# Staging the attention queries on GpSimd in a two-layer hybrid decoder step

## The chip, the cores and the metric

The kernel runs on one core of one Trainium2 chip. A core has five engines that each work through their own list of instructions in order and meet only at semaphores: TensorE (PE in the profile, with its weight loads shown apart as PEld), VectorE (DVE), ScalarE (ACT), GpSimd (POOL) and SyncE (SP), which here issues every DMA. The metric is the device time of one execution in microseconds (us). Lower is better.

## The reference, cut to what matters

One step of a small decoder with two layers: 1024 prompt tokens and 8 sequences of 8 new tokens, model width 1024. The part that matters is the attention of the prompt.

- The first layer has three groups of windowed attention, with 8 heads of 64 features each and dilations 1, 4 and 16. Each group works on blocks of 128 queries against at most 256 keys.
- The second layer has one group with 16 query heads and 4 key heads, the same window of 128, and a sink value per head.

```python
def banded_attn(q, k, v, n_steps):              # blocks of 128 queries
    kb, vb = key_blocks(k), key_blocks(v)       # own block and the one before
    s = einsum('nbqgrd,nbkgd->nbgrqk', qb, kb) * (hd ** -0.5)
    pexp, m, l = _masked_softmax_parts(s, valid)   # exp(s - max), max, sum
    o = einsum('nbgrqk,nbkgd->nbqgrd', pexp, vb)
    return o, m, l
```

Everything else (projections, a state-space layer, the feed-forward parts, the sample attentions) is not touched by the change.

## The kernel before, in words

**Slots.** All weights come as 111 slots of 1.1 MB. For each slot SP loads the raw weights (`feed`, L353), GpSimd splits them into a high and a low part (`split_slot`: a cast on L645, a subtraction on L647), and TensorE multiplies with them. There are two split buffers, so GpSimd's split of slot n waits until TensorE has finished slot n-2. GpSimd does nothing but these splits. SP's load of slot n+1 waits for the end of the split of slot n, since there is one raw buffer.

**The attentions.** The first layer runs, for each of its three groups (g = 0, 1, 2), two value slots, four query and key slots, and then `attend(g, 8 heads)`. The second layer runs `attend(0, 16 heads)` once, after its slot W_VC. An attention goes over 8 tiles of 128 queries. A tile has one step for each pair of heads: 4 steps in the first layer, 8 in the second. In g = 0, in the odd tiles of g = 1 and in the second layer a step sees 256 keys (128 in the first tile); the even tiles of g = 1 and all of g = 2 see 128.

**One step k of a tile, engine by engine.** A query has to be scaled and laid out so that each head's 64 features stand alone among zeros in a 128-row operand. That is the staging: ACT copies 64 x 128 pieces from XA into QST (first layer) or QCST (second), two per step, on L1285, and raises `q_ready`. Then

- PE makes the scores of both heads (L845), raising `s_mm`;
- DVE adds the mask (L1785), takes the negated maximum (L1790) and, in the second layer, takes the minimum with the sink (L1793);
- ACT makes the two exponentials with their sums (L1300);
- PE transposes them (L856), ACT copies the result to SBUF (L1308), and PE multiplies with the values (L870);
- DVE scales the tile's outputs (L1756 to L1758, L1770) and, in the first layer, SP stores them to `og` (L459 to L467).

**The order on each engine is written out by hand.** PE does scores(k), turn(k-2), weigh(k-3), running on into the next tile. ACT does exps(k), then the copy-out of step k-2, then, from the second step on, the staging of step k-1 of the next tile. The last step of a tile is followed by the staging of two steps. A tile's first step therefore begins when PE has the queries of that step, and ACT's stagings stand between two of its exponentials. Before the first tile of an attention ACT stages all steps in a row. A staging waits until PE has made the scores that read the same columns one tile earlier (`late(s_mm, ...)`). In the second layer a head's queries either keep their rows (64 rows to the same 64 rows) or move to the other 64, one of each in every step.

**GpSimd around an attention.** With W_QKV = 2, the slots that follow the query and key slots of group g are 8 + 6g and 9 + 6g. The split of 8 + 6g is done while TensorE still works on the last query and key slot, the split of 9 + 6g starts as soon as that slot is finished, and the split of 10 + 6g waits for the end of the attention and one more slot. In the second layer these are slots 69, 70 and 71.

Of the kernel before, what the change touches and what calls it, by code (L numbers as in the profile page):

```python
# [17 lines left out]
ACT = mybir.ActivationFunctionType  # L18
# [5 lines left out]
HEAD_DIM = 64  # L24
N_STATE = 64
H_A = 8
H_C = 16
# [23 lines left out]
W_U, W_QKV, W_GLU, W_OUT = 0, 2, 20, (21, 69)  # L51
W_FF, W_PLE, W_GATE = (25, 73), (57, 105), (59, 107)
W_QC, W_KC, W_VC, N_SLOTS = 63, 67, 68, 111
# [14 lines left out]
UNITS_AT = [sum(UNITS[:s]) for s in range(N_SLOTS + 1)]  # L68
# [40 lines left out]
def build(nc, a):  # L109
# [14 lines left out]
    with ExitStack() as ctx:  # L124
# [14 lines left out]
        def sem(name):  # L139
            return ctx.enter_context(nc.semaphore(name))  # L140
# [65 lines left out]
        scaled, hi_act, lo_made = sem("scaled"), sem("hi_act"), sem("lo_made")  # L206
        dve_own, act_own = sem("dve_own"), sem("act_own")

        q_ready, s_mm, s_masked, max_made, exp_made = (sem(n) for n in ("q_ready", "s_mm", "s_masked", "max_made", "exp_made"))
        pt_mm, pt_taken, pv_mm, o_made, o_out = (sem(n) for n in ("pt_mm", "pt_taken", "pv_mm", "o_made", "o_out"))  # L210
        turned, zeroed = sem("turned"), sem("zeroed")
# [53 lines left out]
        def prompt_cols(g, i):  # L265

            if g == 0:
                return lambda x: x[:, :, bass.ds(SAMPLE + i * P, P)]
            if g == 1:
                return lambda x: x[:, :, bass.ds(SAMPLE + i[1] * 512 + i[0], P, 4)]  # L270
            return lambda x: x[:, :, bass.ds(SAMPLE + i, P, 8)]
# [368 lines left out]
        @block.gpsimd  # L640
        def _(pool):

            def split_slot(slot, high, low):
                pool.wait_ge(raw_in, 16 * (slot + 1))
                pool.tensor_copy(high[:, :], w_raw[:, :]).then_inc(hi_made, 1)  # L645
                pool.wait_ge(hi_made, slot + 1)
                pool.tensor_tensor(low[:, :], w_raw[:, :], high[:, :].bitcast(F32), ALU.subtract).then_inc(split, 1)  # L647

            for slot in range(N_SLOTS):
                if slot in W_PLE:  # L650
                    pool.wait_ge(lo_made, LO_MIXED[W_PLE.index(slot)] + 24 + 2 * FF_BLOCKS)
                    split_slot(slot, side_hi, side_lo)
                    continue
                if slot >= 2:
                    earlier = slot - 2 - any(slot - 2 <= w < slot for w in W_PLE)
                    pool.wait_ge(slot_done, earlier + 1)
                for layer in range(2):

                    if slot == W_FF[layer] + 1:
                        pool.wait_ge(lo_made, LO_MIXED[layer] + 16)  # L660
                    elif slot == W_GATE[layer]:
                        pool.wait_ge(whole_sum, (5, 14)[layer])
                    elif slot == W_GATE[layer] + 1:
                        pool.wait_ge(lo_made, LO_MIXED[layer] + 24 + 2 * FF_BLOCKS + 24)
                split_slot(slot, w_hi[buffer_of(slot)], w_lo[buffer_of(slot)])
# [3 lines left out]
        def _(pe):  # L669
            u, spl = Units(), Count(split)  # L670
            sqm, rms, lo, added, tsq = Count(sq_made), Count(sums_read), Count(lo_made), Count(part_added), Count(tail_sq)
            n_q, n_s, n_mask, n_exp, n_ptt, n_pt, n_pv, n_o = (
                Count(s) for s in (q_ready, s_mm, s_masked, exp_made, pt_taken, pt_mm, pv_mm, o_made))

            def late(sem_, value):

# [153 lines left out]
            def attend(g, heads, keys, vals):  # L830
# [4 lines left out]
                def tile(i, nk, before, after):  # L835
                    K = key_cols(g, i, nk)(keys)

                    def scores(k):
                        pe.wait_ge(q_ready, n_q.add())
                        m = n_mask.add()  # L840
                        late(s_masked, m - 2)
                        for hh in range(2):
                            h = 2 * k + hh
                            kt = h // 2 if per_kv == 1 else h // 8
                            mm = pe.matmul(psum[:, k % 2, hh * 256:hh * 256 + nk * P], staged[:, h, :], K[:, kt],  # L845
                                           start=True, stop=True)
                        mm.then_inc(s_mm, 1)
# [55 lines left out]
                        if heads == H_C:  # L903
                            outputs_turned()

                per = {n_q: steps, n_mask: steps, n_exp: steps, n_ptt: steps, n_pv: steps, n_o: 1}
                if heads == H_C:
                    per[lo] = 1
                over_tiles(pe, g, per, tile)
                pe.wait_ge(o_made, n_o.at)  # L910

# [298 lines left out]
        def _(act):  # L1210
# [5 lines left out]
            def late(sem_, value):  # L1216

                if not (isinstance(value, int) and value <= 0):
                    act.wait_ge(sem_, value)
# [54 lines left out]
            def attend(g, heads):  # L1274
                steps = heads // 2

                staged = QST if heads == H_A else QCST

                def stage(i, k):

                    late(s_mm, n_s.add() - steps)
                    for par in range(2):
                        rows = 64 * (par if heads == H_A else (k // 2) % 2)
                        q = prompt_cols(g, i)(XA[:, k:k + 1, :])[64 * par:64 * par + 64]
                        mm = act.activation(staged[rows:rows + 64, 2 * k + par:2 * k + par + 1, :], q, ACT.Copy,  # L1285
                                            scale=HEAD_DIM ** -0.5)
                    mm.then_inc(q_ready, 1)

                def tile(i, nk, before, after):
                    if not before:  # L1290
# [1154 lines left out]
```

## Time and profile before

| | before |
|---|---|
| median of 3 runs | 3690.28 us (3689.4 to 3693.12) |
| profiled execution | 3701.41 us, span 3699.6 us |
| granted TensorE clock, mean | 0.948 of full speed |
| PE busy | 3319.2 us (90%) |
| DVE busy | 1402.3 us (38%) |
| ACT busy | 907.2 us (25%) |
| POOL busy | 781.2 us (21%), 226 instructions |

Busy time counts what an engine executes, not what it waits for. Trace times are counted from the start of the span. In a timeline row the columns are start, length, engine, line, operation and operands; a number in brackets is the engine's idle time just before, with what ended it. In a row of windows each engine's busy time is followed by its share or count of instructions, then come the clock that TensorE was granted (1.00 is 2.4 GHz, 0.50 is 1.2 GHz) and the DMA engines' share.

### The profile page before, as it was taken

What the parts mean: (1) busy time and instruction counts of PE and PEld (TensorE: products, weight loads), DVE (VectorE), ACT (ScalarE), POOL (GpSimd) and SP (SyncE); (2) the same over time, 40 slices, a digit from 0 to 9 for tenths busy, and PEclk for the clock granted to TensorE, in tenths of its full rate; (3) what the DMA queues carried; (4) which work ended last, traced back from release to release, by engine and by line L of the source; (5) the groups of instructions that cost most, each with busy time, mean ns of one, the idle gap of its engine ahead of it and who ended that gap; (6) DMA issues with size and microseconds to landing.
All of it is one profiled execution on the core that took longest, in us unless ns stands there. A gap on an engine that the chain in (4) does not pass through costs nothing.

```text
span 3699.6 us, 50510 instructions
## 1 busy us (share of the span) xinstructions
PE 3319.2 (90%) x21025; PEld 3172.0 (86%) x21025; DVE 1402.3 (38%) x1852; ACT 907.2 (25%) x1876; POOL 781.2 (21%) x226
## 2 busy tenths in 40 slices
PE   5978999994467999999999899987899999999988
PEld 4977997983357899999999899976789999999988
DVE  7704013023452443333333753165253333333364
ACT  3106125052031420000000531275142000000051
POOL 2220120210001122222222232200022222222321
PEclk9989999987688999999999999999799999999999
DMA  2221210337941122222225112100112222222411
GB/s 110 93 79 42 91 67 21 120 123 244 288 113 61 37 98 90 85 94 94 94 94 183 41 55 80 54 1 32 61 37 85 79 79 79 79 70 75 164 42 62
DMA packets 84130, 323.03 MB, mean 87 GB/s; under 512 B 19032, under 2 KB 32152, under 8 KB 66072
## 3 DMA queue, kind: packets, MB, share of 16 engines
q1 hardware_dynamic: 84000, 321.18, 25.1%
q8 instruction: 96, 1.57, 0.2%
q14 instruction: 34, 0.28, 0.0%
HBM read 271.98 MB, written 105.23 MB: 102 GB/s over the span
## 4 chain that ended last, share of the span: by engine, by line
PE 78%; DVE 8%; ACT 6%; issue 3%; DMA 2%; SPq 2%; POOL 0%; ACTq 0%; DVEq 0%
PE psum L773 60%; PE psum L798 6%; PE psum L714 2%; PE psum L845 2%; PE psum L870 2%; ACT pr L1300 1%; PE psum L748 1%; DVE stat L1790 1%; ACT pt L1308 1%; DVE xa L1713 1%; DVE sm L1785 1%; DVE rs L1660 1%; SPq L549 1%; DVE h_lo L1650 1%; DMA v_sb<-in_v 1%
## 5 line engine op out<-in xcount | busy, mean ns | idle before, releaser
L645 POOL CAST w_hi<-w_raw 128x2184 fp32r<-128x2184 f32 x109 | 224.8, 2062 | 2840.4 <-PE psum L773 2152.0
L773 PE MATMUL psum<-h_hi,w_hi 128*128 128x364 f32 x2832 | 627.9, 330 | 37.5 <-ACT xa L1258 20.9
L773 PE MATMUL psum<-h_lo,w_hi 128*128 128x364 f32 x2544 | 564.0, 330 | 5.9 <-DVE h_hi L1690 5.9
L647 POOL TENSOR_TENSOR w_lo<-w_raw,w_hi 128x2184 fp32r<-128x2184 f32 x109 | 542.4, 4976 | 8.7
L773 PEld LDWEIGHTS psum<-h_hi,w_hi 128*128 128x128 f32 x2832 | 495.0, 189 | 39.2 <-ACT xa L1258 21.2
L773 PE MATMUL psum<-h_hi,w_lo 128*128 128x364 f32 x2304 | 510.1, 330 | 0.0
L2228 DVE TENSOR_TENSOR xa<-xa,psum 128x1092 f32<-128x1092 f32 x256 | 330.7, 1292 | 382.6 <-PE psum L773 382.4
L773 PEld LDWEIGHTS psum<-h_lo,w_hi 128*128 128x128 f32 x2544 | 442.2, 189 | 6.4 <-DVE h_hi L1690 6.2
L773 PEld LDWEIGHTS psum<-h_hi,w_lo 128*128 128x128 f32 x2304 | 401.0, 189 | 0.0
L1572 ACT ACTIVATE tmp<-tmp 128x1092 f32<-128x1092 f32 x64 | 71.6, 1118 | 1255.6 <-DVE tmp L2212 1255.6
L773 PE MATMUL psum<-hid_hi,w_hi 128*128 128x364 f32 x1536 | 338.6, 328 | 5.4 <-DVE xa L2228 5.4
L773 PE MATMUL psum<-hid_lo,w_hi 128*128 128x364 f32 x1536 | 340.0, 330 | 0.0
L773 PE MATMUL psum<-hid_hi,w_lo 128*128 128x364 f32 x1536 | 339.2, 329 | 0.0
L1785 DVE TENSOR_TENSOR sm<-psum,mask 128x512 f32<-128x512 f32 (+1 forms) x160 | 94.4, 590 | 516.8 <-PE psum L845 513.5
L2212 DVE SCALAR_TENSOR_TENSOR tmp<-psum,sq 128x1092 f32<-128x1092 f32 x64 | 82.7, 1295 | 533.4 <-PE psum L773 508.8
L773 PEld LDWEIGHTS psum<-hid_hi,w_hi 128*128 128x128 f32 x1536 | 267.6, 189 | 6.0 <-DVE xa L2228 6.0
L773 PEld LDWEIGHTS psum<-hid_lo,w_hi 128*128 128x128 f32 x1536 | 267.3, 188 | 0.0
L773 PEld LDWEIGHTS psum<-hid_hi,w_lo 128*128 128x128 f32 x1536 | 266.6, 188 | 0.0
L798 PE MATMUL psum<-w_hi,h_hi 128*128 128x256 f32 x648 | 186.1, 287 | 21.8 <-DVE h_lo L1650 20.1
L798 PE MATMUL psum<-w_hi,h_lo 128*128 128x256 f32 x648 | 184.8, 285 | 0.0
L1300 ACT ACTIVATE pr<-sm,stat 128x256 f32<-128x256 f32 (+1 forms) x320 | 147.1, 460 | 94.9 <-DVE stat L1790 49.7
L798 PE MATMUL psum<-w_lo,h_hi 128*128 128x256 f32 x576 | 164.8, 286 | 0.0
(317 smaller groups left out, 4408.8 us busy)
## 6 DMA issues: line engine op xcount, KB each, us to landing
w_raw<-in_wall SPq DMA_DIRECT2D x111, 1092.0 KB, 5.0
kt_sb<-in_kt SPq DMA_DIRECT2D x16, 1024.0 KB, 10.3
out_ovs<-in_v SPq DMA_DIRECT2D x8, 2032.0 KB, 15.5
x_keep<-xa SPq DMA_DIRECT2D x2, 4368.0 KB, 11.8
xd_late<-x_keep SPq DMA_DIRECT2D x2, 4368.0 KB, 14.0
out_oks<-in_kt SPq DMA_DIRECT2D x8, 1008.0 KB, 8.3
out_ovs<-in_v SPq DMA_DIRECT2D x8, 1008.0 KB, 8.9
og<-o_st SPq DMA_DIRECT2D x24, 264.0 KB, 2.0
```

The lines of the kernel that those rows point to most:

```text
L645: pool.tensor_copy(high[:, :], w_raw[:, :]).then_inc(hi_made, 1)
L647: pool.tensor_tensor(low[:, :], w_raw[:, :], high[:, :].bitcast(F32), ALU.subtract).then_inc(split, 1)
L714: mm = pe.matmul(UNIT[m][:, c, :], w[:, kc, m * P:m * P + P], x[:, kc, c * CH:(c + 1) * CH], start=kc == 0 and w is WH and x is XH, stop=k ...
L773: mm = pe.matmul(UNIT[s][:, c, :], w[:, kc, cols], x[:, kc, c * CH:(c + 1) * CH], start=first, stop=last)
L798: mm = pe.matmul(psum[:, 3 * s + c, 0:256], x[:, kc], w[:, kc, :], start=kc == 0 and x is XH and w is WH, stop=kc == KC - 1 and x is XL)
L845: mm = pe.matmul(psum[:, k % 2, hh * 256:hh * 256 + nk * P], staged[:, h, :], K[:, kt], start=True, stop=True)
L870: mm = pe.matmul(psum[:, 4 + h // 8, (h % 8) * HEAD_DIM:(h % 8 + 1) * HEAD_DIM], pt[:, o:o + P], vals[:, bass.ds(t, 1), c:c + HEAD_DIM], s ...
L1300: mm = act.activation(pr[:, o:o + nk * P], sm[:, o:o + nk * P], ACT.Exp, bias=stat[:, h:h + 1], accum_out=stat[:, 16 + h:17 + h])
L1572: act.activation(TMP[:, m, :], TMP[:, m, :], ACT.Square).then_inc(act_own, 1)
L1785: dve.tensor_tensor(out, psum[:, k % 2, :].rearrange("p (h c) -> p h c", h=2)[:, :, 0:nk * P], m.unsqueeze(1).broadcast_to([P, 2, nk * P]) ...
L2212: dve.scalar_tensor_tensor(chunked(TMP[:, m, :]), UNIT[m], 0.0, chunked(rs2), ALU.max, ALU.mult).then_inc(free[m], 1)
L2228: dve.tensor_tensor(chunked(XA[:, m, :]), chunked(XA[:, m, :]), UNIT[m % 2], ALU.add).then_inc(free[m % 2], 1)
```

## The change

GpSimd takes over stagings from ACT and signals them with a new semaphore `q_pool`.

- In all three groups of the first layer GpSimd stages both heads of every step (two `tensor_scalar` of 64 x 128 per step, 192 in all) and ACT stages nothing.
- In the second layer GpSimd stages the one head of each step that keeps its rows (64 instructions). ACT still stages the one that moves, so PE waits for both semaphores.

GpSimd's instructions stand at two places of its list. Ahead of the split of slot `first + 1` (9, 15, 21 and 70) it waits for the zeroing of the operand and for the eviction of the queries, stages the first tile, waits for its own completion, and then splits the slot. Ahead of slot `first + 2` (10, 16, 22 and 71) it waits for the end of the split just made, and stages tiles 1 to 7; each step waits until PE has made the scores of the same step one tile earlier.

```diff
+            def queries(g, heads, t):
+                steps = heads // 2
+                scored = (8 * g + t - 1) * steps if heads == H_A else N_A_STEPS + (t - 1) * steps
+                i = (t // 2, t % 2) if g == 1 else t
+                for k in range(steps):
+                    if t or g:
+                        pool.wait_ge(s_mm, scored + k + 1)
+                    for par in (range(2) if heads == H_A else ((k // 2) % 2,)):
+                        rows = slice(64 * par, 64 * par + 64)
+                        q = prompt_cols(g, i)(XA[:, k:k + 1, :])[rows]
+                        mm = pool.tensor_scalar((QST if heads == H_A else QCST)[rows, 2 * k + par:2 * k + par + 1, :], q,
+                                                HEAD_DIM ** -0.5, None, ALU.mult)
+                    mm.then_inc(q_pool, 1)
+
+            def queries_around(slot, first, g, heads, n_zeroed):
+                if slot not in (first + 1, first + 2):
+                    return
+                steps, scored = heads // 2, (8 * g * 4 if heads == H_A else N_A_STEPS)
+                pool.wait_ge(split, slot)
+                if slot == first + 1:
+                    pool.wait_ge(zeroed, n_zeroed)
+                    pool.wait_ge(free[0], UNITS_AT[first if heads == H_A else W_KC] // 2)
+                    pool.wait_ge(free[1], UNITS_AT[first if heads == H_A else W_KC] // 2)
+                    queries(g, heads, 0)
+                    pool.wait_ge(q_pool, scored + steps)
+                else:
+                    for t in range(1, 8):
+                        queries(g, heads, t)
+                    pool.wait_ge(q_pool, scored + 8 * steps)
+
             for slot in range(N_SLOTS):
+                for g in range(3):
+                    queries_around(slot, W_QKV + 6 * g + 6, g, H_A, 1)
+                queries_around(slot, W_VC + 1, 0, H_C, 4)
...
                     def scores(k):
-                        pe.wait_ge(q_ready, n_q.add())
+                        pe.wait_ge(q_pool, n_qp.add())
+                        if heads == H_C:
+                            pe.wait_ge(q_ready, n_q.add())
...
                 def stage(i, k):
-                    late(s_mm, n_s.add() - steps)
-                    for par in range(2):
-                        rows = 64 * (par if heads == H_A else (k // 2) % 2)
+                    n_s.add()
+                    if heads == H_C:
+                        late(s_mm, n_s.at - steps)
+                        par, rows = 1 - (k // 2) % 2, 64 * ((k // 2) % 2)
                         q = prompt_cols(g, i)(XA[:, k:k + 1, :])[64 * par:64 * par + 64]
-                        mm = act.activation(staged[rows:rows + 64, 2 * k + par:2 * k + par + 1, :], q, ACT.Copy,
-                                            scale=HEAD_DIM ** -0.5)
-                    mm.then_inc(q_ready, 1)
+                        act.activation(QCST[rows:rows + 64, 2 * k + par:2 * k + par + 1, :], q, ACT.Copy,
+                                       scale=HEAD_DIM ** -0.5).then_inc(q_ready, 1)
```

## Rows read from the trace of the kernel before

**Rows 1.** The page's chain that ended last, shares of the span by engine.
```profile
PE 78%; DVE 8%; ACT 6%; issue 3%; DMA 2%; SPq 2%; POOL 0%; ACTq 0%; DVEq 0%
```

**Rows 2.** Windows over the four attentions: g = 0, 1, 2, then the second layer.
```profile
293.00:395.00 102.00, 87.47 (x568) 77.61 (x569) 48.90 (x96) 66.32 (x224) 5.27 (x2) 0.93 0.11 39
535.00:638.00 103.00, 95.09 (x498) 73.18 (x499) 42.81 (x96) 68.57 (x223) 4.74 (x1) 0.92 0.13 47
778.00:872.00 94.00, 69.26 (x392) 60.99 (x396) 36.24 (x101) 60.74 (x222) 4.47 (x1) 0.70 0.58 175
2386.00:2580.00 194.00, 156.48 (x1040) 137.16 (x1040) 120.34 (x234) 141.90 (x462) 5.53 (x2) 0.95 0.04 13
```

**Rows 3.** Timeline of the start of g = 0; L845 at 299.17 opens tile 1.
```profile
291.45 2.00 POOL L645 CAST w_hi<-w_raw 128x2184 fp32r<-128x2184 f32 x1 [17.00 <-PE psum L773]
292.68 2.58 ACT L1285 ACTIVATE q_st<-xa 64x128 f32<-64x128 f32 x8
293.53 4.82 POOL L647 TENSOR_TENSOR w_lo<-w_raw,w_hi 128x2184 fp32r<-128x2184 f32 x1
...
299.17 1.72 PE L845 MATMUL psum<-xa,q_st 128*128 128x256 f32 x4
```

**Rows 4.** The same for g = 1: ACT's first stagings, and tile 1's first scores.
```profile
534.02 3.56 ACT L1285 ACTIVATE q_st<-xa 64x128 f32<-64x128 f32 x8
...
541.80 2.07 PE L845 MATMUL psum<-xa,q_st 128*128 128x256 f32 x4
```

**Rows 5.** The same for g = 2.
```profile
776.80 3.59 ACT L1285 ACTIVATE q_st<-xa 64x128 f32<-64x128 f32 x8
...
785.03 1.23 PE L845 MATMUL psum<-xa,q_st 128*128 x4
```

**Rows 6.** Timeline: GpSimd's only small instructions, at the start of the program.
```profile
0.25 0.10 POOL L2406 MEMSET const-float32-0.0<- 128x1 f32 x1 [0.25 <-issue]
0.28 0.10 POOL L2406 MEMSET const-float32-1.0<- 128x1 f32 x1
```

**Rows 7.** Stagings on ACT, ns min/median/max: first layer, then second layer.
```profile
L1285 ACT ACTIVATE q_st<-xa x192: 293/420/445, 292.7 to 841.2; 64x128 f32 x120, 64x128 f32<-64x128 f32 x72
L1285 ACT ACTIVATE qc_st<-xa x128: 293/307/310, 2385.3 to 2549.7; 64x128 f32 x80, 64x128 f32<-64x128 f32 x48
```

**Rows 8.** Waits in 293 to 395 us: engine, line, releaser; total us, times, longest.
```profile
ACT pr L1300 <- DVE stat L1790: 18.2, 23, 1.6
```

**Rows 9.** Timeline in g = 1, first step of an even tile.
```profile
555.30 1.75 ACT L1285 ACTIVATE q_st<-xa 64x128 f32<-64x128 f32 x4
...
555.59 0.42 DVE L1790 TENSOR_REDUCE stat<-sm 128x2 f32<-128x256 f32 x1
...
557.07 0.40 ACT L1300 ACTIVATE pr<-sm,stat 128x128 f32<-128x128 f32 x1
```

**Rows 10.** Timeline in g = 2: a tile's first step, then the store wait near its end.
```profile
796.48 0.42 DVE L1790 TENSOR_REDUCE stat<-sm 128x2 f32<-128x256 f32 x1
...
797.05 0.40 ACT L1300 ACTIVATE pr<-sm,stat 128x128 f32<-128x128 f32 x1
...
845.12 0.17 DVE L1756 COPY o_st<-stat 128x8 f32<-128x8 f32 x1 [4.68 <-DMA og<-o_st]
```

**Rows 11.** Timeline in the second layer: step 5 of a tile, then a tile's end.
```profile
2444.20 0.16 DVE L1793 TENSOR_TENSOR stat<-stat,nsink 128x2 f32<-128x2 f32 x1
...
2444.68 0.63 ACT L1285 ACTIVATE qc_st<-xa 64x128 f32 x2
...
2445.34 0.51 ACT L1300 ACTIVATE pr<-sm,stat 128x256 f32<-128x256 f32 x1
...
2453.16 0.17 DVE L1752 TENSOR_TENSOR stat<-stat 128x16 f32<-128x16 f32 x1 [1.10 <-ACT stat L1328]
```

**Rows 12.** Timeline at the second layer's start: GpSimd's split, and DVE beside it.
```profile
2386.82 4.79 POOL L647 TENSOR_TENSOR w_lo<-w_raw,w_hi 128x2184 fp32r<-128x2184 f32 x1
...
2387.94 3.69 DVE L1793 TENSOR_TENSOR stat<-stat,nsink 128x2 f32<-128x2 f32 x1
```

**Rows 13.** Windows after the first tile of g = 0: the granted clock (third from last).
```profile
301.00:303.00 2.00, 2.00 (x9) 1.82 (x8) 1.56 (x5) 0.84 (x3) 0.00 (x0) 0.53 0.80 336
```

More of the change, by code:

```diff
@@ L207, in build @@
         dve_own, act_own = sem("dve_own"), sem("act_own")
+        q_pool = sem("q_pool")
         q_ready, s_mm, s_masked, max_made, exp_made = (sem(n) for n in ("q_ready", "s_mm", "s_masked", "max_made", "exp_made"))
@@ L671, in _ @@
             sqm, rms, lo, added, tsq = Count(sq_made), Count(sums_read), Count(lo_made), Count(part_added), Count(tail_sq)
-            n_q, n_s, n_mask, n_exp, n_ptt, n_pt, n_pv, n_o = (
-                Count(s) for s in (q_ready, s_mm, s_masked, exp_made, pt_taken, pt_mm, pv_mm, o_made))
+            n_q, n_qp, n_s, n_mask, n_exp, n_ptt, n_pt, n_pv, n_o = (
+                Count(s) for s in (q_ready, q_pool, s_mm, s_masked, exp_made, pt_taken, pt_mm, pv_mm, o_made))
             def late(sem_, value):
@@ L904, in tile @@
                             outputs_turned()
-                per = {n_q: steps, n_mask: steps, n_exp: steps, n_ptt: steps, n_pv: steps, n_o: 1}
+                per = {n_qp: steps, n_mask: steps, n_exp: steps, n_ptt: steps, n_pv: steps, n_o: 1}
                 if heads == H_C:
-                    per[lo] = 1
+                    per |= {lo: 1, n_q: steps}
                 over_tiles(pe, g, per, tile)
@@ L1275, in attend @@
                 steps = heads // 2
-                staged = QST if heads == H_A else QCST
                 def stage(i, k):
-                    late(s_mm, n_s.add() - steps)
-                    for par in range(2):
-                        rows = 64 * (par if heads == H_A else (k // 2) % 2)
+                    n_s.add()
+                    if heads == H_C:
+                        late(s_mm, n_s.at - steps)
+                        par, rows = 1 - (k // 2) % 2, 64 * ((k // 2) % 2)
                         q = prompt_cols(g, i)(XA[:, k:k + 1, :])[64 * par:64 * par + 64]
-                        mm = act.activation(staged[rows:rows + 64, 2 * k + par:2 * k + par + 1, :], q, ACT.Copy,
-                                            scale=HEAD_DIM ** -0.5)
-                    mm.then_inc(q_ready, 1)
+                        act.activation(QCST[rows:rows + 64, 2 * k + par:2 * k + par + 1, :], q, ACT.Copy,
+                                       scale=HEAD_DIM ** -0.5).then_inc(q_ready, 1)
                 def tile(i, nk, before, after):
```

## The prediction

> **What bounds the kernel now.** I read the page's chain first: TensorE holds 78% of it, ACT 6%, GpSimd nothing [rows 1]. Most of TensorE's share is the projections and the feed-forward parts, which the change leaves alone. So the change is worth what it is worth inside the four attentions, and there I read one window for each [rows 2]. They last about 102, 103, 94 and 194 us. In none of them is ACT full: it works 65% of g = 0, 67% of g = 1, 65% of g = 2 and 73% of the second layer. GpSimd works 5 us in each, the split of one slot. What sets the pace is a ring: scores on PE, mask and maximum on DVE, exponentials and copy-out on ACT, values on PE, then the scores two steps on. ACT's stagings stand in that ring only where an exponential finds its maximum ready and ACT still staging. The waits show how rare that is in g = 0: 23 of the 32 steps' exponentials stood waiting for DVE, 18.2 us in all [rows 8]. So the 192 x 0.42 and 64 x 0.31 us [rows 7], some 100 us of work taken off ACT, are no measure of the gain. The sum has to be made of the few places where a staging ends last, and of what GpSimd's place in the order costs.
>
> **The cost: tile 1 of each first-layer attention.** GpSimd's new list is: stage tile 0, split slot 9 + 6g, stage tile 1. Before, that split began beside the eviction of the last keys, and ACT staged tile 1 between the exponentials of tile 0. Now tile 1's first query comes only after the whole split. All waiting behind it on PE is everything of the ring, since PE makes the scores of tile 1 before it turns and weighs the last steps of tile 0; ACT and DVE then wait for PE. The split is a cast of 2.00 us and a subtraction of 4.82 us [rows 3], 6.9 us with the 0.08 us between them. I add 0.1 us for each of two hand-overs, taken from that 0.08 us.
>
> The price of one staging on GpSimd is not in the trace. A line through the one-column memset (0.10 us) and the one-input cast (2.00 us for 2184 columns) gives 0.10 + 127 x 1.90/2183 = 0.21 us for 128 columns [rows 3, 6]. The same with the two-input subtraction gives 0.37 us. A staging has one input, so I take 0.25 us, near the cast. In g = 1 and g = 2 it reads every fourth or eighth column; ACT's first eight stagings took 2.58 us in g = 0 and 3.56 us in g = 1 [rows 3, 4], a factor of 1.38, which I carry over: 0.35 us, and 0.51 us at the upper end. The lower end there stays 0.21 us.
>
> Tile 0 can begin staging on GpSimd when it did on ACT, since both wait for the same eviction. Tile 1's first scores then start at that moment plus ten stagings (eight of tile 0, two of the next step), plus 7.1 us:
> - g = 0: 292.68 + 2.5 + 7.1 = 302.3, against 299.17 before [rows 3]: 3.1 us late.
> - g = 1: 534.02 + 3.5 + 7.1 = 544.6, against 541.80 [rows 4]: 2.8 us late.
> - g = 2: 776.80 + 3.5 + 7.1 = 787.4, against 785.03 [rows 5]: 2.4 us late.
>
> Together 8.3 us. With the lower prices it is 5.1 us, with the upper ones 12.7 us. I see nothing that wins it back: after tile 1's first scores the ring runs as before, each step waiting for the one two back. If two stagings of a pair ran side by side (two memsets start 0.03 us apart though each lasts 0.10 [rows 6]), ten would count as five, and the loss would be 3.6 us.
>
> Here a rule of the page weighs in. The Trainium skill (GPSIMD Engine Reference, section Performance pitfalls for Q7 kernels) says that reads with a step of more than 8 bytes cost 2.9 instead of 1.9 cycles per element; g = 1 and g = 2 step by 16 and 32 bytes. By its figures, at its 1.2 GHz, my estimate is 0.20 and 0.31 us, and with the memset's 0.10 us on top 0.30 and 0.41 us, for which the loss would be 10 us in place of 8.3. No row here shows GpSimd on such a read.
>
> **The gain: places where a staging ended last.**
> - g = 0, tiles 1 to 7: none. In the timeline all 28 pairs of exponentials there started within 0.11 us of their maximum, the stagings lying in the waits [rows 8].
> - g = 1: at the first step of an even tile the maximum was ready at 556.01 and ACT staged four pieces until 557.05, so the exponential came at 557.07 [rows 9]. That is 1.06 us; the other two such places have 0.81 and 1.01. Sum 2.9 us.
> - g = 2: the same place is worth 0.15 us at 797.05, since the maximum was ready at 796.90 [rows 10]. Seven places in tiles 1 to 5 have 0.11 to 0.39 us, sum 1.4. What comes faster after that meets a wait of 4.68 us for a store queued behind other loads [rows 10] and is not counted.
> - Second layer: in step 5 of six tiles the exponential came 0.90 to 0.99 us after its maximum, as at 2445.34 [rows 11], because a 1.0 us copy and two stagings stood ahead. One of the two goes: 0.31 us [rows 7], six times 1.9 us. At the end of seven tiles DVE waited 1.1 us for a small exponential of ACT [rows 11] that stands behind a staging. It comes 0.31 us earlier, up to 2.2 us; I take half, since the next step's scores arrive at about the same time. In tile 0 half of 0.36 and 0.51 us. Sum 3.4 us, between 1.9 and 4.5.
>
> Together 7.7 us, between 5 and 9.
>
> **What costs nothing.** In the second layer tile 0's queries are ready long before, since GpSimd is idle while TensorE makes the values; GpSimd's split there runs as before, and the sink step that it held up still waits [rows 12]. Later stagings have a whole tile of 11 us and more for 2 to 3 us of GpSimd work. The split that now ends some 3 us later serves a slot that TensorE needs only after the attention, 90 us on. SP's next load waits for that split, and the tile stores stand behind it in SP's list, but tile 0's outputs are themselves later. Without this cover the cost would be the same 3 us, not another.
>
> **The sum.** 8.3 - 7.7 = +0.6 us. On the profiled 3701.4 us this is 3702.0; the median of the runs shown is 0.997 of that execution, so 3690.9 us, which I give as 3691. The bounds of the terms give 3.6 - 9 = -5 us and 12.7 - 5 = +8 us.
>
> **Rivals.**
> - *GpSimd's small instructions are dear, and the kernel is slower.* The place is tile 1 of the three groups. The loss is -1.2 us + 10 x price + 20 x strided price. The net passes +7.4 us (0.2%) once the contiguous price passes 0.43 us and the strided one 0.6 us. For: the only small GpSimd instruction in the trace is a memset, which reads nothing [rows 6]. Against: cast and subtraction scale to less. At 0.55 and 0.76 us the loss is 19.5 and the net +12: 3702 us.
> - *A shared port.* A sink step of DVE that takes 0.16 us [rows 11] took 3.69 us while GpSimd subtracted, and ended as it ended [rows 12]: an instruction of DVE can be held for the whole of one on GpSimd. The small copies L1756 and L1757 follow the first mask of each tile, and GpSimd's stagings start on the same scores. If each of 16 tiles of g = 1 and g = 2 loses one staging of 0.25 to 0.35 us, that is +4 to +6 us: 3696 us. Against: these copies read one operand, the held instruction two. The Trainium skill (SBUF — State Buffer, section Who interferes with whom) says that copies too can take the pair of ports that GpSimd uses, and that it is an exclusive lock; by that rule, the trace agrees for the two-input case, and no row here shows the copies.
> - *Faster.* The pairs overlap on GpSimd (loss 3.6) and the freed ACT takes all that the chain gave to stagings inside the attentions: about 3 us in g = 1, 5 in g = 2 and 4.5 in the second layer. Net -9: 3681 us. Against: in g = 2 the maxima are ready only 0.1 to 0.4 us earlier [rows 10].
>
> TensorE's clock may move each of these. After tile 0 of g = 0, where PE was sparse, it was granted 0.53 [rows 13], and over g = 2 only 0.70 [rows 2]. A longer gap on PE can lengthen such a stretch by a few us. I count 2 us either way.
>
> **How the numbers follow.** The forecast gets 0.66, dear instructions 0.18, the port 0.08, faster 0.08. A measurement of this kernel can tell about 0.2%, 7.4 us, from no change. The forecast and the port lie inside it, but for a tail of each beyond +7.4, which I give 0.03: same 0.71, slower 0.21, faster 0.08. The range runs from 3684 (the lower bound and the clock) to 3703 (the dear instructions).
>
> **What would show it.** In the trace after: GpSimd's L647 ending about 302 in g = 0, with PE idle for 3 us before tile 1's first scores and the idle put down to GpSimd; the length of one staging; no idle of PE put down to GpSimd in later tiles; exponentials in g = 1 directly behind their maxima; the windows of the three groups longer by about 3, 0 and 1 us, that of the second layer shorter by 3. It would be wrong if PE waited for GpSimd in every tile, or if tiles 1 to 7 of g = 0 became shorter.

## The result, and the profile after

| | before | after |
|---|---|---|
| median of 5 runs each, one chip | 3690.28 us (3684.95 to 3699.80) | 3707.74 us (3706.45 to 3712.31) |
| ratio, 95% interval | | 1.0045 [1.0028, 1.0062] |
| profiled execution, span | 3701.41 us, 3699.6 us | 3712.31 us, 3710.5 us |
| granted clock, mean | 0.948 | 0.942 |

The change makes the kernel slower by 0.45%, 16.6 us (10.3 to 22.9), outside the range I gave. It does what the rival of the dear GpSimd instructions said. First the profile's page of the kernel after: busy times, then the chain by engine, which answers to [rows 1].

```profile
PE 3323.6 (90%) x21025; PEld 3173.3 (86%) x21025; DVE 1403.1 (38%) x1852; ACT 822.7 (22%) x1620; POOL 929.3 (25%) x482
...
PE 78%; DVE 8%; ACT 5%; issue 3%; DMA 3%; SPq 2%; POOL 1%; ACTq 0%; DVEq 0%; POOLq 0%
```

ACT lost 84 us of work and GpSimd took on 148, for the same 256 pieces. GpSimd, which held nothing of the chain, now holds 1%. The groups of GpSimd's stagings, first layer and second (busy us, then mean ns of one; behind the bar the idle time ahead of them):

```profile
L661 POOL TENSOR_SCALAR q_st<-xa 64x128 f32<-64x128 f32 x192 | 116.7, 608 | 141.9 <-PE psum L883 78.5 <-ACT xa L1296 55.2
L661 POOL TENSOR_SCALAR qc_st<-xa 64x128 f32<-64x128 f32 x64 | 33.5, 525 | 119.8 <-PE psum L883 119.1
```

One staging takes 0.525 us where it reads neighbouring columns, not the 0.25 us I had put in. The timeline of g = 0 shows what this does; it answers to [rows 3]. L661 is the staging, L646 and L648 the split, L883 the scores, L1821 the mask, L1792 the first small copy that [rows 10] has as L1756.

```profile
292.98 4.68 POOL L661 TENSOR_SCALAR q_st<-xa 64x128 f32<-64x128 f32 x8 [18.34 <-ACT xa L1296]
...
297.73 2.00 POOL L646 CAST w_hi<-w_raw 128x2184 fp32r<-128x2184 f32 x1
...
299.82 4.79 POOL L648 TENSOR_TENSOR w_lo<-w_raw,w_hi 128x2184 fp32r<-128x2184 f32 x1
...
304.70 4.68 POOL L661 TENSOR_SCALAR q_st<-xa 64x128 f32<-64x128 f32 x8
...
305.86 2.07 PE L883 MATMUL psum<-xa,q_st 128*128 128x256 f32 x4 [5.12 <-POOL q_st L661]
...
307.97 0.69 DVE L1821 TENSOR_TENSOR sm<-psum,mask 128x512 f32<-128x512 f32 x1 [8.02 <-PE psum L883]
...
308.58 0.24 DVE L1792 COPY o_st<-stat 128x8 f32<-128x8 f32 x1
```

Eight stagings take 4.68 us (ACT's eight: 2.58 us), the split stands behind them, two more stagings follow, and only then TensorE can open tile 1, after 5.12 us of idleness put down to GpSimd. The same in g = 1 and g = 2, against [rows 4] and [rows 5]; with every fourth or eighth column read, eight stagings take 5.6 us:

```profile
537.48 5.62 POOL L661 TENSOR_SCALAR q_st<-xa 64x128 f32<-64x128 f32 x8 [18.41 <-ACT xa L1296]
...
551.53 2.16 PE L883 MATMUL psum<-xa,q_st 128*128 128x256 f32 x4 [5.21 <-POOL q_st L661]
```

```profile
784.45 5.67 POOL L661 TENSOR_SCALAR q_st<-xa 64x128 f32<-64x128 f32 x8 [18.41 <-ACT xa L1296]
...
798.74 1.28 PE L883 MATMUL psum<-xa,q_st 128*128 x4 [5.86 <-POOL q_st L661]
```

From these rows and those of before comes the ledger. "To tile 1" runs from the first staging to tile 1's first scores; "whole" from the first staging to the last mask of the attention (for the second layer, first mask to last).

| | to tile 1, before | after | loss | whole, before | after | difference |
|---|---|---|---|---|---|---|
| g = 0 | 6.49 us | 12.88 | +6.4 | 81.39 us | 88.56 | +7.2 |
| g = 1 | 7.78 | 14.05 | +6.3 | 82.73 | 86.82 | +4.1 |
| g = 2 | 8.23 | 14.29 | +6.1 | 74.72 | 79.33 | +4.6 |
| second layer | | | | 180.83 | 175.41 | -5.4 |

Tile 1 loses 18.7 us; behind it 2.9 us come back in the first layer, 2.2 in g = 1 and 1.5 in g = 2, while g = 0 loses 0.8 more. The second layer gains 5.4 us, but 2.4 of it is lost again right after the attention (TensorE's clock, shown below). The sum is 15.9 - 5.4 + 2.4 = +12.9 us, inside the measured 10.3 to 22.9. A second execution of each kernel, shown below, gives 17.4 - 5.5 + 2.8 = +14.7 us by the same reckoning; g = 2 differs most, 71.9 us in place of 74.7 before the change and 77.8 in place of 79.3 after it.

The waits of the kernel after in 293 to 395 us tell the same (columns as in [rows 8]): TensorE waits for GpSimd twice, at the start of tiles 0 and 1, and GpSimd waits for TensorE before the later stagings.

```profile
ACT pr L1336 <- DVE stat L1826: 44.0, 31, 8.5
POOL q_st L661 <- PE psum L883: 35.8, 23, 2.4
...
PE psum L883 <- POOL q_st L661: 7.8, 2, 5.1
```

### The profile page after: what moved, and what is told of

The parts are those of the page before. It is cut to its first block, busy times and chain, and to the rows that moved or that the text cites. A ratio compares the mean times of both kernels' runs of the same rounds, so it can differ in the third digit from the quotient of the medians.

```text
span 3710.5 us, 50403 instructions
## 1 busy us (share of the span) xinstructions
PE 3323.6 (90%) x21025; PEld 3173.3 (86%) x21025; DVE 1403.1 (38%) x1852; ACT 822.7 (22%) x1620; POOL 929.3 (25%) x482
## 4 chain that ended last, share of the span: by engine, by line
PE 78%; DVE 8%; ACT 5%; issue 3%; DMA 3%; SPq 2%; POOL 1%; ACTq 0%; DVEq 0%; POOLq 0%
PE psum L809 59%; PE psum L834 6%; PE psum L883 3%; PE psum L750 2%; PE psum L908 2%; DVE stat L1826 1%; PE psum L784 1%; ACT pr L1336 1%; DVE sm L1821 1%; DVE xa L1749 1%; DMA v_sb<-in_v 1%; DVE h_lo L1686 1%; DVE rs L1696 1%; PE psum L1010 1%; ACT pt L1344 1%
## 5 line engine op out<-in xcount | busy, mean ns | idle before, releaser
L646 POOL CAST w_hi<-w_raw 128x2184 fp32r<-128x2184 f32 x109 | 222.5, 2041 | 2442.0 <-PE psum L809 1458.9
L648 POOL TENSOR_TENSOR w_lo<-w_raw,w_hi 128x2184 fp32r<-128x2184 f32 x109 | 542.5, 4977 | 8.8
L1821 DVE TENSOR_TENSOR sm<-psum,mask 128x512 f32<-128x512 f32 (+1 forms) x160 | 94.5, 590 | 529.5 <-PE psum L883 522.4
```

What stands on the lines that cost most here:

```text
L1821: dve.tensor_tensor(out, psum[:, k % 2, :].rearrange("p (h c) -> p h c", h=2)[:, :, 0:nk * P], m.unsqueeze(1).broadcast_to([P, 2, nk * P]) ...
```

## The experiments

My theory after seeing the trace: tile 1 of the three first-layer groups is late because the split and ten dear stagings stand ahead of it, and the rest is small. Rivals: the loss is somewhere in the second layer or in a port shared with DVE in every tile; and, on the price, whether a GpSimd instruction costs by the piece or by the column.

Each ratio is to runs of the kernel before on the same chip, where its median was 3691.5 to 3693.8 us. The times in the expectations were reckoned from 3690.3 us, so I read them as differences from the kernel before. The diffs are against the changed kernel unless said otherwise and show the deciding lines; the waits of the other engines follow them.

| kernel | median | ratio to before |
|---|---|---|
| second layer alone | 3690.81 us | 0.9991 [0.9981, 1.0002] |
| first layer alone | 3709.76 | 1.0054 [1.0034, 1.0074] |
| tiles 0 and 1 ahead of the split | 3703.95 | 1.0031 [1.0018, 1.0045] |
| ACT stages tile 0 | 3686.61 | 0.9985 [0.9973, 0.9998] |
| ACT stages tile 0 and all of g = 0 | 3688.25 | 0.9985 [0.9970, 1.0000] |
| ACT stages tile 0 and the second layer | 3692.23 | 1.0000 [0.9989, 1.0011] |
| tile 0 in two wide instructions | 3704.87 | 1.0024 [1.0014, 1.0035] |
| the changed kernel again | 3714.82 | 1.0048 [1.0031, 1.0066] |

**One part alone.** The second layer without the first:

```diff
-                for g in range(3):
-                    queries_around(slot, W_QKV + 6 * g + 6, g, H_A, 1)
                 queries_around(slot, W_VC + 1, 0, H_C, 4)
```

> Only the second layer's part of the change: ACT stages everything in the first layer, GpSimd stages the head that keeps its rows in the second. Theory (all of the loss is the late tile 1 of the first layer): the second-layer attention shortens by 5 to 6 us from its first to its last mask, as in the changed kernel's trace, and the whole is 3 to 6 us faster than before, about 3684 to 3687 us. Rival (GpSimd's instructions or the second semaphore slow every step): 3690 us or more.

And the first without the second:

```diff
                 for g in range(3):
                     queries_around(slot, W_QKV + 6 * g + 6, g, H_A, 1)
-                queries_around(slot, W_VC + 1, 0, H_C, 4)
```

> Only the first layer's part: GpSimd stages all of the three dilated groups, ACT both heads in the second layer. Theory: all of the loss and none of the second layer's gain, 3 to 6 us above the changed kernel, about 3710 to 3714 us. Rival (the loss sits in the second layer): about 3690 us.

The second layer alone gives -3.3 us (-7.0 to +0.7), the first alone +19.9 (+12.6 to +27.3). The second layer's attention took 175.36 us in the one and 180.82 in the other; in the second kernel tile 1's first mask came 13.0, 13.4 and 12.8 us after tile 0's in g = 0, 1, 2, as in the changed kernel (12.5, 13.5, 12.8) and not as before (6.8, 7.5, 7.3). The loss is the first layer's.

**Tile 1 ahead of the split.** If the split between tiles 0 and 1 is what costs, putting it behind tile 1 should free it.

```diff
-                    queries(g, heads, 0)
-                    pool.wait_ge(q_pool, scored + steps)
+                    ahead = 2 if heads == H_A else 1
+                    for t in range(ahead):
+                        queries(g, heads, t)
+                    pool.wait_ge(q_pool, scored + ahead * steps)
```

> The changed kernel with one thing moved: in the first layer GpSimd stages tiles 0 and 1 ahead of the split and tiles 2 to 7 behind it. Price of a staging and its number stay. Theory (the split standing between tile 0 and tile 1 is the loss): tile 1's first mask comes 6 to 8 us after tile 0's in place of 12.5 to 13.5, 17 to 18 us of loss go, about 3684 to 3692 us; what is left of the loss is tile 0's late start, 1.1 + 0.5 + 0.7 us. Rival (the price of GpSimd's instructions is lost in every tile, or a shared port slows DVE): 3700 us or more. If tile 2 is late because the split now stands ahead of its stagings, its first mask shows it.

I missed this one: tile 1 is on time (6.1, 7.4 and 6.7 us after tile 0), but only about a third of the loss goes, by ratios whose intervals overlap. Its timeline in g = 0 shows why. Here L885 is the scores, L1794 the small copy, L1828 the maximum; SPq rows are DMA issues.

```profile
305.83 4.83 POOL L648 TENSOR_TENSOR w_lo<-w_raw,w_hi 128x2184 fp32r<-128x2184 f32 x1
...
310.69 0.33 SPq L354 DMA_DIRECT2D w_raw<-in_wall  x1
310.75 5.89 POOL L661 TENSOR_SCALAR q_st<-xa 64x128 f32<-64x128 f32 x10
...
311.23 0.34 SPq L460 DMA_DIRECT2D og<-o_st  x1
312.13 0.91 PEld L885 LDWEIGHTS psum<-xa,q_st 128*128 128x128 f32 x4 [0.53 <-issue]
...
317.65 0.17 DVE L1794 COPY o_st<-stat 128x8 f32<-128x8 f32 x1 [3.05 <-DMA og<-o_st]
318.03 0.69 DVE L1828 TENSOR_REDUCE stat<-sm 128x2 f32<-128x512 f32 x1
318.83 0.51 ACT L1338 ACTIVATE pr<-sm,stat 128x256 f32<-128x256 f32 x1 [6.41 <-DVE stat L1828]
```

The split now ends at 310.66. Tile 2's first query comes behind it, and SP's load of the next slot, which waits for that split, goes out at 310.69 with the store of tile 0's outputs behind it at 311.23. DVE waits 3.05 us for that store before it may overwrite the outputs, and ACT stands 6.41 us behind DVE. Tile 2 lasts 14.3 us in place of 11.2. So moving the split moves the loss, and takes SP's queue along.

**Leave tile 0 to ACT.** Then GpSimd can split when it did before, while ACT stages, and has all of tile 0 to get to tile 1. The first edit is GpSimd's, the second ACT's, where `first` is true for the steps of an attention's first tile; TensorE waits for the engine that stages.

```diff
-                if slot not in (first + 1, first + 2):
+                if slot not in ((first + 2,) if heads == H_A else (first + 1, first + 2)):
...
-                    if heads == H_C:
+                    if heads == H_C or first:
```

> ACT stages tile 0 of each first-layer attention as before, GpSimd splits at the old moment and stages tiles 1 to 7; the second layer as in the changed kernel. Theory: no late start of tile 0, tile 1 late by 0.4 us at most in g = 0 (split ends 298.4, two stagings of 0.58), and the gains stay (2 to 3 us in g = 1, 1 in g = 2, 3 to 6 in the second layer): 3681 to 3687 us. Rival (dear instructions or the port in every tile): 3695 us or more.

```profile
294.25 2.59 ACT L1324 ACTIVATE q_st<-xa 64x128 f32<-64x128 f32 x8
...
295.11 4.82 POOL L648 TENSOR_TENSOR w_lo<-w_raw,w_hi 128x2184 fp32r<-128x2184 f32 x1
...
300.01 4.09 POOL L661 TENSOR_SCALAR q_st<-xa 64x128 f32<-64x128 f32 x7
...
301.18 1.73 PE L884 MATMUL psum<-xa,q_st 128*128 128x256 f32 x4 [0.56 <-POOL q_st L661]
```

TensorE's wait for GpSimd at tile 1 shrinks from 5.12 to 0.56 us, and the kernel is faster than the kernel before, though by little: 0.9985 [0.9973, 0.9998]. With tile 0 staged by ACT and the split at its old place, the same stagings in all other tiles cost nothing that can be measured. The loss came from GpSimd's order around tile 0, and the price of a staging gave its size.

**Is the rest of the first layer worth moving?** Two more kernels, with diffs against the last one, leave g = 0, or the second layer, to ACT as well:

```diff
-                for g in range(3):
+                for g in (1, 2):
                     queries_around(slot, W_QKV + 6 * g + 6, g, H_A, 1)
```

> The version with ACT staging tile 0 of each first-layer group, which took 3686.6 us, but with all of g = 0 staged by ACT as before the change; GpSimd stages tiles 1 to 7 of g = 1 and g = 2 and the second layer's heads that keep their rows. Theory: g = 0 has nothing to gain from the freed ACT, and GpSimd's stagings there cost about 0.1 us a tile beside DVE's small copies (0.24 us in place of 0.16), so its tiles come back to 11.15 us from 11.26 and the time falls by 0.5 to 1 us: 3685 to 3687 us. Rival: GpSimd's stagings in g = 0 did gain something that the tile starts hide, and the time rises to 3688 or more.

```diff
                 for g in range(3):
                     queries_around(slot, W_QKV + 6 * g + 6, g, H_A, 1)
-                queries_around(slot, W_VC + 1, 0, H_C, 4)
```

> ACT stages tile 0 of each first-layer group and GpSimd tiles 1 to 7 after the split, as in the version that took 3686.6 us, but the second layer's queries all stay on ACT. Two questions. First, what the first layer alone brings: by the tile starts of that version g = 0 loses 1 us, g = 1 gains 2.4 and g = 2 gains 3.0, so -4.4 us, 0.9988 of before; rival: the gains are clock, and the ratio is 1.000. Second, whether TensorE's clock after the second layer's attention goes with that attention's stagings: in the profiles so far the first 4 us after its last mask ran at 1.00 in the two kernels whose second layer is staged by ACT and at 0.50 in the six in which GpSimd takes half. If it goes with the stagings, this one shows 1.00 and 92 to 97 us from the last mask to the split of slot 71; if it was chance, 0.50 and 99 us or more is as likely.

With g = 0 on ACT its tiles are back at 11.15 us from 11.25, so GpSimd's stagings cost a tile there 0.1 us and win nothing; the ratio stays at 0.9985, too small a step to be told in the time. The first layer alone brings nothing that can be measured: my -4.4 us is just outside its interval (-4.1 to +4.1). Of its terms the 3.0 us of g = 2 can't be told from chance: a second execution of the kernel before (below) has 69.6 us from g = 2's first mask to its last, not 72.4, and this kernel has 69.4. That g = 1 gains holds in both: 80.4 and 80.8 before, 77.4 here.

**What one staging costs.** Other forms of staging inside one run of the changed kernel:

```diff
-                        q = prompt_cols(g, i)(XA[:, k:k + 1, :])[rows]
-                        mm = pool.tensor_scalar((QST if heads == H_A else QCST)[rows, 2 * k + par:2 * k + par + 1, :], q,
-                                                HEAD_DIM ** -0.5, None, ALU.mult)
+                        q = prompt_cols(0 if (g == 2 and t % 2) else g, i)(XA[:, k:k + 1, :])[rows]
+                        n = (128, 128, 64, 32, 16, 8, 128, 128)[t] if g == 0 and heads == H_A else 128
+                        out = (QST if heads == H_A else QCST)[rows, 2 * k + par:2 * k + par + 1, 0:n]
+                        if g == 1:
+                            mm = pool.tensor_copy(out, q)
+                        else:
+                            mm = pool.tensor_scalar(out, q[:, :, 0:n], HEAD_DIM ** -0.5, None, ALU.mult)
```

> Measures the price of one GpSimd staging. It is the changed kernel with other forms of staging inside one run: in g = 0 the eight tiles stage 128, 128, 64, 32, 16, 8, 128 and 128 columns of each query block (the rest of the block keeps older values), in g = 1 the staging is a plain copy without the scale, and in g = 2 the odd tiles read 128 neighbouring columns instead of every eighth. So part of the queries and of the scaling is left out; the times of the rest are unchanged. In the profile of the changed kernel a pair took 1.11 to 1.17 us in g = 0 and 1.36 us with a stride. Theory A, a fixed cost for each small instruction: a pair of 8 columns still takes 0.8 us or more, and the pairs between lie on a line with at most 0.4 us for 128 columns. Theory B, a price for each column, as my line from the cast assumed in kind: a pair of 8 columns takes 0.3 us or less. On the form: if the multiplication is what is dear, the copies of g = 1 take under 1.2 us a pair; if not, 1.36 us as before. On the stride: the odd tiles of g = 2 take 1.11 to 1.17 us a pair, the even ones 1.36.

GpSimd's groups of this run, first g = 0 by shape, then the copies of g = 1:

```profile
L666 POOL TENSOR_SCALAR q_st<-xa 64x128 f32<-64x128 f32 x32 | 16.8, 525 | 34.1 <-ACT xa L1300 18.3 <-PE psum L887 14.2
L666 POOL TENSOR_SCALAR q_st<-xa 64x64 f32<-64x64 f32 x8 | 2.9, 364 | 3.7 <-PE psum L887 3.3
L666 POOL TENSOR_SCALAR q_st<-xa 64x32 f32<-64x32 f32 x8 | 2.3, 284 | 8.2 <-PE psum L887 8.0
L666 POOL TENSOR_SCALAR q_st<-xa 64x16 f32<-64x16 f32 x8 | 2.0, 248 | 9.1 <-PE psum L887 8.9
L666 POOL TENSOR_SCALAR q_st<-xa 64x8 f32<-64x8 f32 x8 | 1.8, 228 | 9.3 <-PE psum L887 9.0
...
L664 POOL COPY q_st<-xa 64x128 f32<-64x128 f32 x64 | 25.9, 405 | 60.9 <-PE psum L887 40.8 <-ACT xa L1300 18.4
```

These lie on a line: (525 - 228) / 120 = 2.5 ns for each column and 0.21 us for the instruction. Each theory has a part: a pair of 8 columns took 0.52 us, between the 0.8 us of the one and the 0.3 us of the other, and of the 0.525 us the columns are 0.32. The stride adds 0.12 us: in g = 2 the odd tiles (neighbouring columns) took 1.11 us a pair and the even ones 1.36. The form counts too: a strided copy took 0.405 us, a strided multiplication by a constant 0.65.

**Fewer, wider instructions for tile 0.** Two of 64 x 512 in place of eight of 64 x 128:

```diff
+                if heads == H_A and t == 0:
+                    if g:
+                        pool.wait_ge(s_mm, scored + steps)
+                    for par in range(2):
+                        rows = slice(64 * par, 64 * par + 64)
+                        mm = pool.tensor_scalar(QST[rows, par::2, :], prompt_cols(g, i)(XA[:, 0:steps, :])[rows],
+                                           HEAD_DIM ** -0.5, None, ALU.mult)
+                    mm.then_inc(q_pool, steps)
+                    return
```

> The changed kernel, but GpSimd stages tile 0 of each first-layer group with two instructions of 64 x 512 instead of eight of 64 x 128; everything else, the split's place too, as in the changed kernel. Theory A (a fixed cost of about 0.45 us for each instruction, and 0.13 us more for 128 columns, 0.25 us with a stride): tile 0 takes 2 x (0.45 + 0.52) = 1.9 us in g = 0 and 2 x (0.45 + 1.0) = 2.9 us in g = 1 and 2, where eight took 4.7 and 5.6. Tile 1 starts 2.7 us earlier than in the changed kernel in each group, but the first scores wait for all eight heads and not for two, 0.8 to 1.5 us later than there; as tile 1 is what sets the time, some 8 us of 16.6 come back: 3698 to 3703 us. Theory B (a price for each column): tile 0 takes as long as before, 4.7 and 5.6 us, its first scores come 3.5 us later and nothing comes back: 3707 to 3712 us.

```profile
294.84 3.03 POOL L660 TENSOR_SCALAR q_st<-xa 64x512 f32<-64x512 f32 x2 [18.34 <-ACT xa L1305]
...
306.09 2.08 PE L892 MATMUL psum<-xa,q_st 128*128 128x256 f32 x4 [2.62 <-POOL q_st L670]
```

Tile 0's staging fell from 4.68 to 3.03 us here and by 1.7 us in g = 1 and 2, and tile 1's first mask, counted from the first staging, came 1.6, 1.7 and 1.6 us earlier: what GpSimd saves ahead of the split arrives at tile 1 in full. That is 4.9 us in all, smaller than theory A's 2.8 us a group, since 512 columns cost by the column. The ratio fell to 1.0024 from the 1.0048 of the changed kernel on the same chip, 8.9 us, but the two intervals overlap, so the time can't tell how much came back. The time itself lies above theory A's range; as a difference, +8.9 us, it lies within.

**Both kernels again, and TensorE's clock.** The changed kernel once more:

> The changed kernel as it is, a second time, for a second profiled execution and a closer ratio. Expected by the theory (tile 1 of each first-layer group waits for the split and ten dear stagings; what the profiled execution gave back after g = 0 was TensorE's clock and not the change): 3705 to 3711 us, tile 1's first mask again 5 to 6 us later after tile 0's than before in all three groups, and the value slot after g = 0 at either clock level. Rival (the give-back after g = 0 belongs to the change): that slot runs at 1.00 again, and so it does in every kernel with the same list of GpSimd in the first layer, and at 0.50 in the kernel before.

And the kernel before:

> The kernel before, a second time, for a second profiled execution. The first showed the value slots after g = 0 and after g = 1 at half the clock for 9 us, 4.2 us each; seven other kernels showed that in two of seven cases after g = 0 and one of seven after g = 1. If this is chance of the execution, one or both are at full clock here and the span is 3691 to 3696 us; if it belongs to the kernel before, both are at half clock again and the span is 3699 us. After the second layer's attention: 1.00 in the first 4 us and 92 to 97 us to the split of slot 71 if that goes with ACT's stagings.

The changed kernel's loss (+17.7 us by its ratio) and its tile 1 (13.0, 13.4 and 12.9 us after tile 0) came again. The kernel before took 3690.0 us in its second profiled execution, 11.4 us less than in its first and below the span I expected. Of that, 4.1 us lie behind g = 0 and 4.2 behind g = 1, both by TensorE's clock, and 2.8 in g = 2. Windows behind g = 0 of its first execution, where the attention's last mask is at 374.07, and of its second, last mask at 375.32 (columns as in [rows 2]):

```profile
374.00:378.00 4.00, 2.85 (x25) 2.40 (x24) 1.72 (x5) 2.95 (x9) 0.00 (x0) 1.00 0.17 68
378.07:382.07 4.00, 4.00 (x21) 4.00 (x21) 0.00 (x0) 0.60 (x1) 0.00 (x0) 0.50 0.00 0
```

```profile
375.32:379.32 4.00, 2.84 (x24) 2.40 (x23) 1.73 (x5) 2.89 (x9) 0.00 (x0) 1.00 0.17 68
379.32:383.32 4.00, 3.15 (x28) 3.01 (x28) 0.69 (x1) 0.60 (x1) 0.00 (x0) 1.00 0.00 0
```

TensorE did the same before, 2.85 and 2.84 us of work in 4, and was then granted 1.2 GHz in one execution and 2.4 GHz in the other. At 1.2 GHz the stretch from the last mask to the next split lasted 37.4 us in place of 33.2. Over the profiles of this case that happened behind g = 0 or g = 1 in nine places of 24, with no pattern by kernel. So the give-back of 4.1 us that the first profile of the changed kernel shows there is not the change's; it is why its profiled execution is only 10.9 us above the first one of before.

Behind the second layer's attention it is otherwise. My expectations call it the first 4 us after the last mask; it is the second four. The kernel before, last mask at 2567.85, then the kernel after, last mask at 2576.56:

```profile
2567.85:2571.85 4.00, 2.68 (x23) 2.21 (x21) 2.14 (x6) 3.01 (x10) 0.00 (x0) 1.00 0.02 6
2571.85:2575.85 4.00, 2.63 (x25) 2.49 (x24) 1.22 (x1) 0.60 (x1) 0.00 (x0) 1.00 0.00 0
```

```profile
2576.56:2580.56 4.00, 2.68 (x22) 2.21 (x20) 2.14 (x6) 3.00 (x10) 0.00 (x0) 0.98 0.01 4
2580.56:2584.56 4.00, 4.00 (x21) 4.00 (x21) 0.00 (x0) 0.60 (x1) 0.00 (x0) 0.50 0.00 0
```

In all four profiles in which ACT stages the second layer these second four microseconds ran at 2.4 GHz, in all eight in which GpSimd takes half they ran at 1.2. From the last mask to the split of slot 71 it took 94.8 to 95.4 us in the four and 97.2 to 97.6 in the eight. So 2 to 3 us of the 5.4 go back there each time, 2.4 in the first two profiles. The lower clock comes in all twelve, but in the four it comes some 4 us later. That it goes with the stagings is shown; why the shorter attention meets the slower clock is not, as TensorE's work in the last 12 us before is the same in both.

The clock also lies inside the 5.4 us. In tile 6 of this attention, 141.4 us after its first mask, the same four profiles have 3.4 us at 1.2 GHz, and the eight have none. The masks of steps 1 and 2 of that tile, before and then after:

```profile
2530.35 0.69 DVE L1785 TENSOR_TENSOR sm<-psum,mask 128x512 f32<-128x512 f32 x1 [3.15 <-PE psum L845]
...
2533.63 0.68 DVE L1785 TENSOR_TENSOR sm<-psum,mask 128x512 f32<-128x512 f32 x1
```

```profile
2540.28 0.69 DVE L1821 TENSOR_TENSOR sm<-psum,mask 128x512 f32<-128x512 f32 x1 [1.96 <-PE psum L883]
...
2542.96 0.68 DVE L1821 TENSOR_TENSOR sm<-psum,mask 128x512 f32<-128x512 f32 x1
```

The step lasts 3.28 us before and 2.68 after. In tiles 2 to 5 of the kernel before, at 2.4 GHz, it lasts 2.69, and the step ahead of it 3.86 in place of tile 6's 4.76. So some 1.5 us of the 5.4 come by the clock, and 3.9 are left for the stagings themselves.

## Why the prediction was wrong

**The place was right, and so was the sum's form.** I had the split and ten stagings ahead of tile 1's first scores. With the measured prices, 5.9 us for ten stagings in g = 0 (4.68 for eight, 0.07 between, 1.16 for two) and 7.1 in the others, in place of my 2.5 and 3.5, my own sum gives 305.7, 548.2 and 791.0 us. Taking off how much later the eviction ended in this execution (0.2, 3.3 and 7.5 us), tile 1's first scores came at 305.7, 548.2 and 791.2.

**The step that failed is the price of one staging.** I drew a line through a memset of one column and the cast of 2184 and read 0.21 us off it, took 0.25, and set the two-input subtraction as upper end, 0.37 us, since a staging has one input. The run of widths shows both parts of that line to be wrong: 0.21 us for the instruction where the memset gave 0.10, and 2.5 ns for each column where the cast has 0.87 and the subtraction 2.2. A multiplication by a constant costs more for each column than the subtraction of two tensors, so what I took for an upper end was below the value. Start to start it is 0.59 us and, strided, 0.71. The loss at tile 1 was 18.7 us, against 8.3 forecast and an upper end of 12.7.

**The stride** I took from ACT, a factor of 1.38; on GpSimd it is 0.65 to 0.525 us, 1.23. The Trainium skill (GPSIMD Engine Reference, section Performance pitfalls for Q7 kernels) prices it at one cycle more for each element, by its 1.2 GHz an estimate of 0.11 us for 128; the trace agrees, with 0.12. Its 1.9 cycles for an element without a stride, 1.6 ns, lie below the 2.5 ns measured here for the multiplication.

**The gains.** g = 0: none, as said, and 0.8 us lost. g = 1: 2.2 us for 2.9, and as I had said the exponential of an even tile's first step now follows its maximum at once, where [rows 9] has 1.06 us between:

```profile
565.42 0.42 DVE L1826 TENSOR_REDUCE stat<-sm 128x2 f32<-128x256 f32 x1
...
565.95 0.40 ACT L1336 ACTIVATE pr<-sm,stat 128x128 f32<-128x128 f32 x1 [0.71 <-DVE stat L1826]
```

g = 2: 1.5 us for 1.4 by these two profiles, but by the second profile of before it can't be told from nothing. Second layer: 5.4 us in the attention for 3.4, of which 1.5 came by the clock in tile 6, and 3.0 net once the clock has taken 2.4 behind it. That the net lies so near the forecast is in part luck: the clock moved it both ways, and I had looked at step 5 and at a tile's end, while the masks show a gain of 0.6 us a tile (tiles 2 to 5) that arises at the first, second and last-but-one step.

**What I said costs nothing** did cost nothing in the changed kernel: TensorE waits for GpSimd at the later tiles only twice, 0.20 and 0.16 us in g = 2, though a tile's stagings took 4.7 to 5.7 us and not 2 to 3; and SP's late load adds no wait for a store. The kernel with both tiles ahead of the split shows how little cover that was: the split some 5 us later still, and a store behind SP's load holds DVE for 3 us in each group.

**The rivals.** The dear instructions are what happened: 0.59 and 0.71 us lie beyond the 0.43 and 0.6 from which that rival decides, and its formula, -1.2 + 10 x 0.59 + 20 x 0.71, gives 18.9 us, where tile 1 lost 18.7. Its net of 12 us, from somewhat other prices, is near the ledger's 12.9. A shared port is at most small: L1792 takes 0.24 us at 308.58, while GpSimd stages, for the 0.17 of [rows 10], so it isn't held for the length of a staging. In g = 1 and g = 2, where that rival put its loss, no such copy took longer than 0.30 us, and all 32 together took 0.8 us more than before, not 4 to 6. The tiles of g = 0 lose 0.1 us each; that this is the copies' is argued, not shown. The clock, for which I had allowed 2 us either way, moved 4.1 us by execution alone behind g = 0. The chance of 0.18 for dear instructions was too low for a price of which no row showed the operation.

What stays open: the ledgers have +12.9 and +14.7 us and the ratios +16.6 and +17.7; the ledgers lie inside the ratios' intervals, but no more than that. The clock in and behind the second layer's attention is open too.

## What to carry to other kernels

When work moves to an engine that is idle, look at what already stands in that engine's list at the moment when the first piece is wanted: here a split of 6.9 us between tile 0 and tile 1 of each first-layer attention made a slower kernel of stagings that cost nothing elsewhere, and leaving only the first tile where it was made a slightly faster one. A price for an operation that the trace doesn't have is not bounded by other operations of that engine, even by one that reads more; the range has to reach to where the sign turns. And busy time freed on an engine that is not full is no gain: 84 us off ACT bought some 3 us net in the second layer and 2 in g = 1.

## What was not expected of the hardware

- GpSimd's multiplication by a constant, float32: 0.21 us and 2.5 ns for each column (8 to 128 columns of 64 rows; two of 512 took 3.03 us), 0.65 us for 128 strided columns. Its strided copy of the same took 0.405 us.
- TensorE's granted clock behind an attention differs between two executions of one kernel, 0.50 or 1.00, at 4.1 us each. With the second layer's stagings it went by kernel: 4 to 8 us behind the last mask it was 0.50 in all eight profiles in which GpSimd staged half of the queries and 1.00 in the other four, and a stretch of 3.4 us at 0.50 in tile 6 was in those four alone.
